# The key/value latent and the rotary key of an input projection computed as two blocks of 288 columns

## The reference

```
u = rms_norm(h, norm_mix_g[i]) @ w_in[i]            # 2048 -> 1024 + 512 + 512 + 64
y_pool = multiscale_pool(u[..., :1024], pool_w[i], pool_scale[i])
y_att = latent_attention(u[..., 1024:1536],         # c_q
                         u[..., 1536:2048],         # c_kv, key/value latent
                         u[..., 2048:],             # rotary key, 64 columns
                         cos, sin, q_norm_g[i], w_uq[i], kv_norm_g[i], w_ukv[i])
h = h + concatenate([y_pool, y_att]) @ w_out[i]
```

## Time and profile before

| | |
|---|---|
| Median of 3 runs | 2291.21 us (2286.39 to 2292.51) |
| Span of the profiled execution, first to last instruction | 2290.0 us |
| TensorE busy | 2251.6 us |
| VectorE busy | 1393.2 us |
| ScalarE busy | 1050.4 us |
| Mean granted TensorE clock | 0.986 |

### The profile page before, as it was taken

One profiled execution on the slowest core, in us unless ns is written; L12 is line 12 of the kernel. 1 busy time (PEld: TensorE's weight loads), 2 busy tenths in 40 slices (PEclk: granted clock), 3 DMA queues, 4 the chain that ended last, 5 costly groups with the idle time before them and its releaser, 6 DMA issues.

```text
span 2290.0 us, 31512 instructions
## 1 busy us (share of the span) xinstructions
PE 2251.6 (98%) x10594; PEld 1880.8 (82%) x10594; DVE 1393.2 (61%) x1768; ACT 1050.4 (46%) x1349; POOL 67.1 (3%) x152
## 2 busy tenths in 40 slices
PE   7999999999999999999999999999999999999997
PEld 5898888888888888888878988888888888888886
DVE  6457655656666565666454675566565666656755
ACT  5346544444444444446453455444444444444553
POOL 7000000000000000000000000000000000000000
PEclk8899999999999999999998999999999999999998
DMA  6553555555555556545554445555555555555562
GB/s 216 150 145 129 203 193 180 185 181 201 183 183 181 185 166 203 199 166 199 168 176 134 139 162 185 188 180 192 183 174 194 192 187 185 170 199 165 184 219 76
DMA packets 233598, 406.60 MB, mean 178 GB/s; under 512 B 19033, under 2 KB 46121, under 8 KB 233385
## 3 DMA queue, kind: packets, MB, share of 16 engines
q1 hardware_dynamic: 232041, 401.87, 52.7%
q0 software_dynamic: 656, 2.63, 0.3%
q10 hardware_dynamic: 816, 1.05, 0.2%
HBM read 403.42 MB, written 2.10 MB: 177 GB/s over the span
## 4 chain that ended last, share of the span: by engine, by line
PE 96%; issue 1%; DVE 1%; ACT 1%; DMA 0%; SPq 0%; DVEq 0%; ACTq 0%; POOLq 0%; POOL 0%
PE acc L1404 31%; PE acc L1406 31%; PE acc L1405 31%; PE tps L1461 3%; DMA raw<-in_w_in 0%; PE tps L1405 0%; PE tps L1406 0%; PE tps L1404 0%; DVE w_lo L1000 0%; ACT w_hi L605 0%; PE tps L1648 0%; DVE h L1387 0%; DVE xa_lo L1011 0%; DVE sg L1354 0%; DVE h L1359 0%
## 5 line engine op out<-in xcount | busy, mean ns | idle before, releaser
L1000 DVE TENSOR_TENSOR w_lo<-raw,w_hi 128x1024 fp32r<-128x1024 f32 x770 | 925.3, 1233 | 514.7 <-ACT w_hi L822 355.2
L822 ACT ACTIVATE w_hi<-raw 128x1024 fp32r<-128x1024 f32 x508 | 525.8, 1059 | 512.2 <-PE acc L1406 512.2
L1404 PE MATMUL acc<-w_hi,xa_hi 128*128 128x512 f32 (+1 forms) x1792 | 704.0, 393 | 11.7 <-DVE w_lo L1000 7.8
L1405 PE MATMUL acc<-w_hi,xa_lo 128*128 128x512 f32 (+1 forms) x1792 | 699.6, 390 | 0.0
L1406 PE MATMUL acc<-w_lo,xa_hi 128*128 128x512 f32 (+1 forms) x1792 | 699.5, 390 | 0.0
L1404 PEld LDWEIGHTS acc<-w_hi,xa_hi 128*128 128x128 f32 x1792 | 345.0, 193 | 79.8 <-issue 10.0
L1406 PEld LDWEIGHTS acc<-w_lo,xa_hi 128*128 128x128 f32 x1792 | 344.9, 192 | 68.9
L1405 PEld LDWEIGHTS acc<-w_hi,xa_lo 128*128 128x128 f32 x1792 | 345.3, 193 | 67.3
L605 ACT ACTIVATE w_hi<-raw 128x1024 fp32r<-128x1024 f32 x262 | 268.2, 1063 | 154.7 <-PE acc L1406 144.9
L1404 PE MATMUL acc<-w_hi,gt_hi 128*128 128x512 f32 x640 | 254.7, 398 | 0.0
L1405 PE MATMUL acc<-w_hi,gt_lo 128*128 128x512 f32 x640 | 253.1, 395 | 0.0
(11 more groups left out here) (202 smaller groups left out, 1365.2 us busy)
## 6 DMA issues: line engine op xcount, KB each, us to landing
raw<-in_w_up SPq DMA_DIRECT2D x176, 1024.0 KB, 5.1
raw<-in_w_down SPq DMA_DIRECT2D x88, 1024.0 KB, 5.1
raw<-in_w_in SPq DMA_DIRECT2D x32, 1024.0 KB, 5.3
raw<-in_w_out SPq DMA_DIRECT2D x32, 1024.0 KB, 5.1
raw<-in_w_ple_gate SPq DMA_DIRECT2D x32, 1024.0 KB, 5.1
raw<-in_w_ukv SPq DMA_DIRECT2D x8, 1024.0 KB, 5.6
raw<-in_w_uq SPq DMA_DIRECT2D x6, 1024.0 KB, 5.9
raw<-in_w_ple SPq DMA_DIRECT2D x4, 1024.0 KB, 5.0
```

The costliest lines, as they stand in the source:

```text
L822: copy(w_hi[:, half_of(m), :], raw[:, c % RAW_SLOTS, (m % 2) * HALF:(m % 2 + 1) * HALF], ACT.Copy).then_inc(hi_done, 1)
L1000: dve.tensor_tensor(w_lo[:, half_of(m), :], raw[:, c % RAW_SLOTS, (m % 2) * HALF:(m % 2 + 1) * HALF], w_hi[:, half_of(m), :].bitcast(F32), ...
L1404: pe.matmul(dst, a_hi, b_hi, start=first, stop=False)
L1405: pe.matmul(dst, a_lo, b_hi, start=False, stop=False)
```

## The change

The 576 columns of `ckv` and `kr` are cut in the middle. `LW` is 288; the first block (still named `ckv`) has columns 0 to 287 of the 576, the second (`kr`) columns 288 to 575, that is the last `KVR` = 224 of the latent and the 64 rotary ones. Each is loaded in three chunks of 6, 6 and 4 row blocks (`LATE`), in place of four chunks of 4 row blocks and one of 16, so a half is 3 or 2 row blocks of 288 columns (864 or 576 columns), and the two blocks have 6 halves each. The two loads of `poolw` become one of 1 MB, of which each half serves one pair of groups. A layer has 26 chunks ahead of `out` as before.

```
-    for name, n in (("cq", per_block), ("ckv", per_block), ("kr", 1), ("pool", 2 * per_block), ("uq", 3),
-                    ("ukv", 4), ("poolw", 2), ("out", n_blk * per_block), ...
+    for name, n in (("cq", per_block), ("ckr", 6), ("pool", 2 * per_block), ("uq", 3),
+                    ("ukv", 4), ("poolw", 1), ("out", n_blk * per_block), ...
...
+    LW = (LORA + ROPE) // 2
+    KVR = LORA - LW
...
+        def span(m):
+            i = m // 2 - CH["ckr"]
+            n = LATE[i % len(LATE)] // 2 * LW if 0 <= i < 2 * len(LATE) else HALF
+            return (m % 2) * n, n
...
+                for col in (D_POOL + LORA, D_POOL + LORA + LW):
+                    k0 = 0
+                    for nk in LATE:
+                        load(l, c, (rows(w_in, l, k0, nk, col, LW), nk * LW, LW))
+                        k0, c = k0 + nk, c + 1
```

Both splits take only `n` columns at `at` (`at, n = span(m)`). On TensorE:

```
-                square_halves(l, m, b, xa, 0, 4)
+                def late_half(i, blk):
+                    hi, lo = halves(l, 2 * CH["ckr"] + 6 * blk + i)
+                    b = BL["ckv"] + blk
+                    if i == 0:
+                        free_acc(l, b)
+                    nk = LATE[i // 2] // 2
+                    kt = sum(LATE[:i // 2]) + (i % 2) * nk
+                    for k in range(kt, kt + nk):
+                        cols = slice((k - kt) * LW, (k - kt + 1) * LW)
+                        for t in range(TT):
+                            tok = slice(t * P, (t + 1) * P)
+                            ins = three(acc[b % 2][:, t, 0:LW], xa[0][:, k, tok], xa[1][:, k, tok], hi[:, cols],
+                                        lo[:, cols], k == 0, k == KT - 1)
+                    ins.then_inc(w_used, 1)
+                for i in range(4):
+                    late_half(i, 0)
...
                 turn_lat(0, JB["cq"])
-                square_halves(l, m, b, xa, 4, 8)
...
+                for i in range(4, 6):
+                    late_half(i, 0)
+                for i in range(6):
+                    late_half(i, 1)
                 m, b = 2 * CH["pool"], BL["pool"]
-                square_halves(l, m, b, xa, 0, 2)
+                square_halves(l, m, b, xa, 0, 5)
                 pe.wait_ge(kr_step, 3 * l + 3)
...
                 turn_lat(1, JB["ckv"])
-                square_halves(l, m, b, xa, 2, 8)
+                square_halves(l, m, b, xa, 5, 8)
```

On ScalarE the latent is copied out in two parts, and the rotary key comes with the second:

```
-                steps(l, 12, 16)
-                latent(1)
-                steps(l, 16, 18)
-                b = BL["kr"]
+                steps(l, 12, 14)
+                b = BL["ckv"]
                 block_ready(act, l, b)
                 for t in range(TT):
-                    ins = copy(kr_in[:, t, :], acc[b % 2][:, t, 0:ROPE], ACT.Copy,
-                               scale=rstd["mix"][:, t:t + 1])
-                    ins.then_inc(acc_free[b % 2], 1)
-                steps(l, 18, 20)
+                    copy(lat[:, 1, t, 0:LW], acc[b % 2][:, t, 0:LW], ACT.Copy,
+                         scale=rstd["mix"][:, t:t + 1]).then_inc(acc_free[b % 2], 1)
+                steps(l, 14, 20)
+                latent(1)
+                steps(l, 20, 26)
```

`latent(1)` now waits for the second block, copies its last 64 columns to `kr_in` (a new semaphore, `kr_out`), then the 224 others to `lat`, then sums the squares of all 512. VectorE waits for `kr_out` ahead of the rotary steps, splits two halves, scales the latent, and splits four more:

```
-                steps(l, 12, 18)
-                latent(1)
-                dve.wait_ge(acc_free[BL["kr"] % 2], BLOCKS * l + 2 * (BL["kr"] // 2 + 2))
+                steps(l, 12, 20)
+                dve.wait_ge(kr_out, TT * l + TT)
...
-                steps(l, 18, 20)
+                steps(l, 20, 22)
+                latent(1)
+                steps(l, 22, 26)
```

More of the change, by code:

```diff
@@ L48 @@
 BLK = 512
+LATE = (6, 6, 4)
 T_BANKS = 4
@@ L76, in layer_plan @@
     last = {}
-    for name, n in (("cq", 1), ("ckv", 1), ("pool", 2)):
+    for name, n in (("cq", 1), ("pool", 2)):
         for i in range(n):
             last[block[name] + i] = 2 * (chunk[name] + (i + 1) * per_block) - 1
-    last[block["kr"]] = 2 * chunk["kr"]
+    last[block["ckv"]] = 2 * chunk["ckr"] + 5
+    last[block["kr"]] = 2 * chunk["ckr"] + 11
     last[block["qrope"]] = 2 * chunk["uq"] + 1
@@ L85, in layer_plan @@
     for i in range(2):
-        last[block["poolw"] + i] = 2 * (chunk["poolw"] + i)
+        last[block["poolw"] + i] = 2 * chunk["poolw"] + i
     for name, ends in (("out", (11, 15, 23, 31)), ("ffn", (7, 15, 23, 31, 33, 35, 37, 39)),
@@ L366, in _ @@
                 c = CH["cq"]
[L367 to L372, removed]
+                for k in range(KT // 4):
+                    load(l, c, square(w_in, l, k, D_POOL))
+                    c += 1
+                for col in (D_POOL + LORA, D_POOL + LORA + LW):
[3 more added lines that the diff above has]
+                        k0, c = k0 + nk, c + 1
                 for col in (0, BLK):
@@ L384, in _ @@
                         c += 1
[L385 to L388, removed]
+                load(l, c, (pool_w[bass.ds(l, 1)].rearrange("l g (k p) n -> p (l g k) n", p=P), CHUNK, 2 * P))
+                c += 1
                 for j, k in ([(j, k) for k0 in (0, 2) for j in (0, 1) for k in (k0, k0 + 1)]
@@ L604, in split @@
                 act.wait_ge(w_used, l * (2 * CHUNKS) + m + 1)
-                copy(w_hi[:, half_of(m), :], raw[:, c % RAW_SLOTS, (m % 2) * HALF:(m % 2 + 1) * HALF],
-                     ACT.Copy).then_inc(hi_done, 1)
+                at, n = span(m)
+                copy(w_hi[:, half_of(m), 0:n], raw[:, c % RAW_SLOTS, at:at + n], ACT.Copy).then_inc(hi_done, 1)
             def steps(l, a, b):
@@ L671, in latent @@
                         act.wait_ge(rstd_done, 5 * l + 2)
-                    for t in range(TT):
-                        copy(lat[:, i, t, :], acc[b % 2][:, t, :], ACT.Copy,
-                             scale=rstd["mix"][:, t:t + 1]).then_inc(acc_free[b % 2], 1)
+                        for t in range(TT):
+                            copy(lat[:, i, t, :], acc[b % 2][:, t, :], ACT.Copy,
+                                 scale=rstd["mix"][:, t:t + 1]).then_inc(acc_free[b % 2], 1)
+                    else:
+                        for t in range(TT):
+                            copy(kr_in[:, t, :], acc[b % 2][:, t, KVR:LW], ACT.Copy,
+                                 scale=rstd["mix"][:, t:t + 1]).then_inc(kr_out, 1)
+                        for t in range(TT):
+                            copy(lat[:, i, t, LW:LORA], acc[b % 2][:, t, 0:KVR], ACT.Copy,
+                                 scale=rstd["mix"][:, t:t + 1]).then_inc(acc_free[b % 2], 1)
                     for t in range(TT):
@@ L702, in _ @@
                     gained(l, JB["ckv"] + i, xb, LAT_KV + 2 * i, G_KV + 2 * i, lat_hi)
-                steps(l, 20, 26)
+                steps(l, 26, 28)
                 def pooled(i):
@@ L747, in _ @@
                          ACT.Copy).then_inc(qr_hi, 1)
-                steps(l, 44, 46)
+                steps(l, 46, 48)
                 for i in range(2):
@@ L756, in _ @@
                         whole(l, b, t, v[0][:, t, i * BLK:(i + 1) * BLK], v_hi)
-                steps(l, 46, 48)
+                steps(l, 48, 50)
                 def pool_rows(n):
@@ L1130, in _ @@
                     dve.wait_ge(qr_step, 3 * TT * l + 3 * t + 3)
-                steps(l, 36, 38)
+                steps(l, 38, 40)
                 def qk(b, kt, number):
@@ L1491, in _ @@
                         turn_h(l, JB["mix"], 5 + 2 * i)
-                m, b = 8, BL["ckv"]
-                square_halves(l, m, b, xa, 0, 4)
+                def late_half(i, blk):
[7 more added lines that the diff above has]
+                        cols = slice((k - kt) * LW, (k - kt + 1) * LW)
+                        for t in range(TT):
+                            tok = slice(t * P, (t + 1) * P)
[4 more added lines that the diff above has]
+                    late_half(i, 0)
                 def turn_lat(i, job):
@@ L1654, in pool_out @@
                     b = BL["poolw"] + i
-                    hi, lo = halves(l, 2 * (CH["poolw"] + i))
+                    hi, lo = halves(l, 2 * CH["poolw"] + i)
                     free_acc(l, b)
```

64 lines of the change are left out of this document (25 added, 39 removed).

## The result

The changed kernel takes 2256.7 us (median of 4, 2255.5 to 2258.5) against 2291.9 us before (median of 4, 2286.4 to 2293.1). The ratio is 0.9854, with a 95% interval of 0.9841 to 0.9868. By that ratio it is 33 us faster; the two medians lie 35.2 us apart. The profiled execution took 2256.0 us, with a span of 2254.4.

The account below looks back on a forecast made before the run. TensorE, busy for 98% of the span, was taken to bound the kernel. The span of 2290.0 us less 30.1 (15.1 and 15.0 by layer) is 2259.9, plus 1.2 to the median: 2261.1 us, range 2252 to 2271.

Parts of the forecast that it names:

- The mechanism: In `kr`, 64-column matmuls cost 111.5 ns at full clock, 213.4 at half; 288 columns throughout save 30.1 us.
- Pace of 288 columns: In both new blocks, a 288-column matmul takes 133.2 ns, between ends of 119.8 and 226.7.
- The saving of the stage: The two late blocks before the pool block get shorter by 15.0 us in layer 0, 15.1 in layer 1.
- The full clock: In the changed stage of both layers the granted clock stays at 1.00, as in rows of 256 and 512 columns.
- The rule against it: For `kr`, the skill's gap of 25 ns at 64 columns makes it 2.4 us, so nothing would be gained.
- Splits and order: On ScalarE and VectorE, splits keep up with TensorE and the new order makes it wait nowhere.
- cover: Time to spare before TensorE wants a result in layer 1's changed stage: 2.7, 5.9 and 6.0 us at three places.
- Loads: Late loads of 864 or 576 KB land in under 5.9 us, against 4.8 of use; no cost taken.
- the unused splits that go save nothing: Dropping the unused second halves of `kr` and the pool weights saves nothing, as neither ScalarE nor VectorE binds.
- the line on `poolw`: One 1 MB load leaves two halves less to split ahead of the first head; TensorE's matmuls there stay the same.
- The pool block of layer 1: Its start comes 27 to 29 us earlier than 1215.9: 15 from layer 0, 13 from its own layer.

Follow-up runs that it names:

- experiment 1: Kernel before, each of the 96 `kr` matmuls moving 256 or 128 columns in place of 64: 2276.2 and 2273.5 us, against 2290.6 before.
- experiment 3: Changed kernel with its cut moved to 448 + 128, 384 + 192 or 320 + 256 columns: 2266.2, 2262.2 and 2257.2 us; unmoved again, 2258.1.
- experiment 4: Kernel before, `kr`'s weights 64 tokens wide in place of 128, so 192 matmuls of 64 columns: 2276.2 us, a single run, against 2290.4.
- experiment 2: Changed kernel with its order and loads, cut moved back to 512 and 64 columns: 2285.7 us, ratio 0.9982 to the kernel before.
- experiment 6: Kernel before, unused halves split over 16 columns only: 2288.6 us; kernel before, two splits moved ahead of the first head's softmax: 2293.2 us.
- experiment 5: Kernel before, `kr`'s 64-column matmuls dealt out among the pool block's first three halves, transposes later: 2292.6 us, ratio 1.0030.

## Why the prediction was right

- **The mechanism.** Confirmed by its own terms. A floor of 111 ns, which goes with the width of the weights, leaves 64 columns mostly unfilled (experiments 1, 3, 4), the clock falls in that block (experiments 1, 2), and wider matmuls do away with both. 128 columns separate the two without touching the rest: the block still costs its floor, but keeps the clock. That alone is worth 17 us in the runs; in the traces it is 16.3 (17.0 + 1.8 and 16.7 + 2.2 us before, 10.7 a layer with 128 columns). Another 14.1 are the floor: 96 × (226.7 + 111.1) ns = 32.4 us a layer at full clock against 192 × 132.1 = 25.4. Together they are the 30.4 us of the two stages. The rest is at the start, the heads and the border. Why the clock falls in the thin block is not shown: the runs tell with which matmuls it fell and with which it did not. The prediction said nothing of it either; it took the full clock from its rows of 256 and 512 columns.
- **Pace of 288 columns.** 132.1 ns for 133.2.
- **The saving of the stage.** 15.2 us in each layer for 15.0 and 15.1.
- **The full clock.** 1.00 in both layers.
- **The rule against it.** 64, 128 and 192 columns at 111 ns leave the gap of 25 ns at 64 columns that the Trainium skill gives (TensorE: Matmul & The Clock Gate, section Back-to-back issue gap) a factor of four too low here. That section calls its formula the isolated gap and says that it has no budget for the weight load at few columns, so it was never the price of this block; the prediction left that out. The rule of the same page's section LDWEIGHTS in the Trainium skill, P / 1.2, gives 107 and 53 ns for 128 and 64 columns of weights; the runs have 111 and 58.
- **Splits and order.** No new wait of TensorE. So no cover that the prediction worked out fell short.
- **Loads.** 4.8 us for 864 KB, within the bound of 5.9.
- **What was missed.** 4.4 us, 2256.7 for 2261.1. The step "the unused splits that go save nothing" and the line on `poolw` took the waits at the heads for fixed; they are worth 0.9 us. The border of the layers was not in the sum at all: in the seven profiled kernels with the old order VectorE starts its loop's first split 3.5 to 3.9 us late, in the six with the new one 2.1 to 3.0. It lies between the loop's branch and the first instruction of the next pass; why that takes longer in one order than in the other is open, as no experiment touched it. The fall of the clock there (1.7 us) appears in three of those seven and none of those six, so it may be partly chance. The start differs from run to run of the same kernel by more than its 0.9 us: in a second profile of the changed kernel the rotary key's transposes in layer 0 came 2.1 us later. So of the 4.4 us the 0.9 at the heads belong to the change, and part of the border's too: TensorE's wait there is 0.7 to 1.8 us in the six profiles with the new order and 1.9 to 2.6 in the seven with the old. The rest may be chance.
- The pool block of layer 1 began 33.0 us earlier (1182.86 for 1215.88), not 27 to 29, by the same 5 us.

## What to carry to other kernels

A matmul that moves few columns with weights of its own has a floor that goes with the width of the weights: here 64, 128 and 192 columns cost the same 111 ns. Before adding a thin block, see whether its columns can be shared out with a neighbour, at an equal count of matmuls, so that both parts lie above that floor; where exactly the cut falls then made no difference here (0.2 us between 288 + 288 and 320 + 256). Look at the granted clock in the block, and behind it too: here a long run of thin matmuls cost twice, by its floor and by the clock, at a TensorE that the page shows as fully busy.

## What the runs showed of the hardware

- The granted clock fell to 0.50 in every unbroken run of 96 matmuls of 64 columns with 128-column weights, some 3 to 6 us after its start, TensorE wholly busy (two stretches each in four kernels: the one before, experiment 2 and both of experiment 6). In the same place it fell in none of the seven profiles with 128 columns or more, and not with 64-column weights, at 58 ns a matmul. Elsewhere it fell among 512-column matmuls too: at the start, and behind a wait of TensorE of 1.9 to 2.5 us at the border of the layers (three of thirteen profiles).
- The lower clock held for 30.7 us through a mixture that ran at full clock in the other layer (experiment 5).
- VectorE's first split of its loop's second pass began 2.1 to 3.9 us after its work before had ended, with ScalarE's first split already done in the two traces shown, and kernels of one order agree in it within a microsecond. Before, 4.3 us lay between the loop's branch and the next pass's first instruction, after the change 3.0.
